# A decoder layer's attention: two heads' rotated scores side by side, and its rounds moved

## The reference

```
q = concatenate([q[..., :128], rope(q[..., 128:], positions)])
k = concatenate([k[..., :128], rope(k[..., 128:], positions)])
for j in range(4):                      # blocks of 128 queries, keys up to their end
    sc = einsum("bqhd,bkhd->bhqk", q[:, 128j:128j+128], k[:, :128j+128]) * 192 ** -0.5
    sc = where(k_chunk <= q_chunk, sc, -inf)          # chunks of 64
    out_j = softmax(sc) @ v[:, :128j+128]
```

## Time and profile before

| | us |
|---|---|
| median of three runs (2251.33 to 2252.22) | 2251.95 |
| the profiled execution, its own time | 2247.52 |
| its span, first to last instruction | 2245.6 |
| TensorE busy in the span | 2184.4 |
| attention rounds, 2093.3 to 2180.0: length, TensorE, VectorE, ScalarE | 86.7, 84.7, 66.4, 50.9 |
| output projection and store, 2180.0 to 2245.6: length, TensorE, VectorE | 65.6, 61.4, 31.2 |

### The profile page before, as it was taken

The page is one execution under the profiler, slowest core; times in us unless marked ns, Lnnn a source line. Parts: engine busy times, 40 slices in busy tenths (PEclk is TensorE's granted clock), DMA queues, the critical chain, the costliest instruction groups (busy, mean ns, idle before and its releaser), DMA issues. The chain is left out here.

```text
span 2245.6 us, 31402 instructions
## 1 busy us (share of the span) xinstructions
PE 2184.4 (97%) x11300; PEld 1575.4 (70%) x11300; DVE 1676.4 (75%) x2154; ACT 1392.2 (62%) x1805; POOL 341.0 (15%) x158
## 2 busy tenths in 40 slices
PE   8998989999999999999999999999999999999999
PEld 8987775556556555555556555677797787887777
DVE  6455658898898998898988998756655556885664
ACT  5344456777777777777777777754555455675553
POOL 3033130211220212220212200320000000320000
PEclk9999989999999999999999999999999999999999
DMA  6212349999999999999999999522221131131301
GB/s 183 78 58 94 110 171 343 371 383 384 375 378 375 373 382 384 373 381 376 374 383 387 367 382 373 206 81 89 80 71 57 57 136 37 51 134 38 113 1 38
DMA packets 179654, 506.85 MB, mean 226 GB/s; under 512 B 12541, under 2 KB 57373, under 8 KB 179565
## 3 DMA queue, kind: packets, MB, share of 16 engines
q1 hardware_dynamic: 174813, 494.92, 59.2%
q0 software_dynamic: 4752, 10.75, 2.2%
HBM read 492.99 MB, written 10.48 MB: 224 GB/s over the span
## 5 line engine op out<-in xcount | busy, mean ns | idle before, releaser
L2010 DVE TENSOR_TENSOR pieces_low<-pieces,pieces_high 128x2048 fp32r<-128x2048 f32 x383 | 873.3, 2289 | 110.5 <-ACT pieces_high L1958 105.7
L1958 ACT ACTIVATE pieces_high<-pieces 128x2048 fp32r<-128x2048 f32 x381 | 727.1, 1916 | 238.9 <-PE ps L1882 238.8
L1882 PE MATMUL ps<-pieces_high,ex_x 128*66 128x512 f32 x2080 | 575.9, 394 | 1.9 <-DVE ex_x L2044 1.5
L1882 PEld LDWEIGHTS ps<-pieces_high,ex_x 128*66 128x66 f32 x2080 | 279.9, 137 | 195.9 <-issue 6.9
L1882 PE MATMUL ps<-pieces_low,ex_x 128*66 128x512 f32 x1040 | 324.1, 393 | 0.0
L1882 PE MATMUL ps<-pieces_high,ex_h 128*66 128x512 f32 x992 | 277.4, 394 | 0.0
L483 DVE TENSOR_TENSOR in_w<-ring,in_w 128x256 fp32r<-128x256 f32 (+3 forms) x284 | 135.2, 483 | 161.6 <-ACT in_w L470 159.6
L2321 PE MATMUL ps<-hn_split,in_w 128*128 128x512 f32 (+1 forms) x888 | 227.3, 406 | 5.8 <-DVE hn_split L483 3.2
L1882 PEld LDWEIGHTS ps<-pieces_low,ex_x 128*66 128x66 f32 x1040 | 141.9, 136 | 97.7 <-issue 0.8
L470 ACT ACTIVATE in_w<-ring 128x256 fp32r<-128x256 f32 (+3 forms) x284 | 118.4, 419 | 131.9 <-PE ps L2321 58.6
L1882 PEld LDWEIGHTS ps<-pieces_high,ex_h 128*66 128x66 f32 x992 | 133.7, 136 | 90.7 <-DVE pieces_low L2010 3.2
(11 more groups left out here) (477 smaller groups left out, 2754.7 us busy)
## 6 DMA issues: line engine op xcount, KB each, us to landing
pieces<-in_w_gate SPq DMA_DIRECT2D x128, 1024.0 KB, 7.3
pieces<-in_w_up SPq DMA_DIRECT2D x128, 1024.0 KB, 7.5
pieces<-in_w_down SPq DMA_DIRECT2D x128, 1024.0 KB, 8.8
ring<-in_a_w_in SPq DMA_DIRECT2D x24, 1024.0 KB, 5.1
ring<-in_w_in SPq DMA_DIRECT2D x8, 1024.0 KB, 5.0
ring<-in_b_w_in SPq DMA_DIRECT2D x4, 2048.0 KB, 7.8
ring<-in_b_w_out SPq DMA_DIRECT2D x2, 3072.0 KB, 14.0
ring<-in_w_in SPq DMA_DIRECT2D x8, 512.0 KB, 3.5
```

Of the source, the lines that this page charges most:

```text
L1882: ins = pe.matmul(ps[0:CAP, banks + c, :], parts[a][:, k0 + k, :], w[b][:, k, c * 512:(c + 1) * 512], start=start and k == 0 and a == b == ...
L1958: nc.scalar.activation(m.high[:, n % NSPLIT, :], m.pieces[:, n % NPIECE, :], ACT.Copy).then_inc(high_done, 1)
L2010: nc.vector.tensor_tensor(m.low_part[:, n % NSPLIT, :], m.pieces[:, n % NPIECE, :], m.high[:, n % NSPLIT, :].bitcast(F32), ALU.subtract).t ...
```

## The change

- `qpt` has one tile per two heads, without zero rows; its clearing and the waits for that are gone, and `take_turned_pe` is one copy of 128 partitions.
- The causal units are ordered by two heads, then tile, then head of the two, so that units 2q and 2q+1 have the same tile of neighbouring heads. In an even round TensorE issues both plain scores, in the odd round after it both rotated scores, on 64 rows each, one on partitions 0 to 63 and one on 64 to 127; only these raise `scored`.
- There are four banks for scores (0, 1, 2, 7), and six buffers of weights. `turn` comes at u-4 instead of u-3, `values` at u-5 instead of u-4, `take` at u-6 instead of u-5, ScalarE's copy at u-4.
- The first three output splits are in rounds 33, 37 and 41 instead of 44, 46 and 48. Step 0 of the projection comes at the end of round 49, step 1 in round 50 before `values`, step 2 at the end of round 51, the rest last.

```diff
@@ -2144,16 +2144,16 @@
             final.g.pool_lows(pool)
 
 
-def attention_stage(m, name, units, at, y, x, out_slots, store):
+def attention_stage(m, name, units, at, st_at, y, x, out_slots, store):
 
 
 
     nc, ps = m.nc, m.ps
 
-    NB = 5
+    NB = 6
     probs = m.area(f"{name}_probs", [P, NB, 512], at)
     pt = m.area(f"{name}_pt", [P, 2, 512], at + 2048 * NB)
-    st = m.area(f"{name}_st", [P, NB, 4], at + 2048 * (NB + 2))
+    st = m.area(f"{name}_st", [P, NB, 4], st_at)
     scored = m.sem(f"{name}_scored")
     maxed = m.sem(f"{name}_maxed")
     exped = m.sem(f"{name}_exped")
@@ -2164,15 +2164,17 @@
     taken = m.sem(f"{name}_taken")
     nu = len(units)
 
-    whole = {k: [(taken, 16 + 4 * (k + 1))] for k in range(BH)}
-    bank_waits = {u % 3: [(exped, u + 1)] for u in range(nu - 3, nu)}
+    score_banks = (0, 1, 2, 7)
+    bank_of = lambda u: score_banks[u % 4]
+    whole = {k: [(taken, 16 + 8 * (k // 2 + 1))] for k in range(BH)}
+    bank_waits = {bank_of(u): [(exped, u + 1)] for u in range(nu - 4, nu)}
     bank_waits.update({i: [(pt_ready, nu)] for i in (3, 4)})
     bank_waits.update({i: [(taken, nu)] for i in (5, 6)})
     out = out_gemm(m, "out3", y, x, TILES2, out_slots, whole, banks=8,
-                   bank_order=[7] + [u % 3 for u in range(nu - 3, nu)] + [3, 4, 5, 6],
+                   bank_order=[bank_of(u) for u in range(nu - 4, nu)] + [3, 4, 5, 6],
                    bank_waits=bank_waits)
 
-    split_at = {nu - 4 + 2 * i: i for i in range(out.ns)}
+    split_at = {nu - 15 + 4 * i: i for i in range(out.ns)}
 
     with nc.Block() as block:
         @block.sync
@@ -2183,13 +2185,19 @@
         @block.tensor
         def _(pe):
             def scores(u):
-                if u >= 3:
-
-                    pe.wait_ge(exped, u - 2)
-                for i, (lhs, rhs) in enumerate(units[u]["scores"]):
-                    ins = pe.matmul(ps[:, u % 3, 0:units[u]["width"]], lhs, rhs,
-                                    start=(i == 0), stop=(i == len(units[u]["scores"]) - 1))
-                ins.then_inc(scored, 1)
+
+                if u >= 4:
+                    pe.wait_ge(exped, u - 3)
+                lhs, rhs = units[u]["scores"]
+                alone = "turned" not in units[u]
+                ins = pe.matmul(ps[:, bank_of(u), 0:units[u]["width"]], lhs, rhs, start=True, stop=alone)
+                if alone:
+                    ins.then_inc(scored, 1)
+
+            def turned_scores(u):
+
+                lhs, rhs = units[u]["turned"]
+                pe.matmul(ps[:, bank_of(u), 0:units[u]["width"]], lhs, rhs, start=False, stop=True).then_inc(scored, 1)
 
             def turn(u):
                 pe.wait_ge(ready, u + 1)
@@ -2210,16 +2218,26 @@
                                     start=(s == 0), stop=(s == len(vs) - 1))
                 ins.then_inc(summed, 1)
 
-            for u in range(nu + 4):
-                if u < nu:
+            for u in range(nu + 5):
+                if u < nu and "turned" not in units[u]:
                     scores(u)
-                if 3 <= u < nu + 3:
-                    turn(u - 3)
-                if u >= 4:
-                    values(u - 4)
-                if u == nu:
+                elif u < nu and u % 2 == 0:
+                    scores(u)
+                    scores(u + 1)
+                elif u < nu:
+                    turned_scores(u - 1)
+                    turned_scores(u)
+                if 4 <= u < nu + 4:
+                    turn(u - 4)
+                if u == nu + 2:
+                    out.products(pe, start=1, stop=2)
+                if u >= 5:
+                    values(u - 5)
+                if u == nu + 1:
                     out.products(pe, stop=1)
-            out.products(pe, start=1)
+                if u == nu + 3:
+                    out.products(pe, start=2, stop=3)
+            out.products(pe, start=3)
 
         @block.vector
         def _(dve):
@@ -2228,7 +2246,7 @@
             def head(u):
                 w = units[u]["width"]
                 dve.wait_ge(scored, u + 1)
-                s = ps[:, u % 3, 0:w]
+                s = ps[:, bank_of(u), 0:w]
                 if units[u]["mask"] is not None:
                     step(nc.vector.tensor_tensor(s[:, w - P:w], s[:, w - P:w], units[u]["mask"], ALU.add))
                 nc.vector.tensor_reduce(st[:, u % NB, 0:1], s, AX.X, ALU.max, negate=True).then_inc(maxed, 1)
@@ -2245,11 +2263,11 @@
                 y = units[u]["y"]
                 nc.vector.tensor_tensor(y, ps[:, 5 + u % 2, 0:P], y, ALU.mult).then_inc(taken, 1)
 
-            for u in range(nu + 5):
+            for u in range(nu + 6):
                 if u < nu:
                     head(u)
-                if u >= 5:
-                    take(u - 5)
+                if u >= 6:
+                    take(u - 6)
                 if 1 <= u <= nu:
                     norm(u - 1)
                 if u in split_at:
@@ -2258,10 +2276,10 @@
 
         @block.scalar
         def _(act):
-            for u in range(nu + 3):
-                if u >= 3:
-
-                    n = u - 3
+            for u in range(nu + 4):
+                if u >= 4:
+
+                    n = u - 4
                     w = units[n]["width"]
                     act.wait_ge(turned, n + 1)
                     if n >= 2:
@@ -2273,7 +2291,7 @@
                     act.wait_ge(maxed, u + 1)
                     if u >= NB:
                         act.wait_ge(turned, u - NB + 1)
-                    nc.scalar.activation(probs[:, u % NB, 0:w], ps[:, u % 3, 0:w], ACT.Exp,
+                    nc.scalar.activation(probs[:, u % NB, 0:w], ps[:, bank_of(u), 0:w], ACT.Exp,
                                          bias=st[:, u % NB, 0:1], accum_out=st[:, u % NB, 1:2]).then_inc(exped, 1)
                 if u in split_at:
                     out.highs(act, split_at[u])
...
@@ -3238,9 +3255,9 @@
                     nc.scalar.activation(qt[:, 2 * c + i, :], ps[:, 5 + i, :], ACT.Copy, scale=m.col("q_nope"))
 
             def take_turned_pe(c):
-                act.wait_ge(cleared, 1 if c == 0 else 2)
-                nc.scalar.activation(qpt[0:64, 2 * c, :], ps[0:64, 7, :], ACT.Copy)
-                nc.scalar.activation(qpt[64:128, 2 * c + 1, :], ps[64:128, 7, :], ACT.Copy).then_inc(q_taken, 1)
+                if c == 2:
+                    act.wait_ge(*used_after(QUP + NB - 1))
+                nc.scalar.activation(qpt[:, c, :], ps[:, 7, :], ACT.Copy).then_inc(q_taken, 1)
 
             def squares_mq():
                 act.wait_ge(*taken(MQ))
@@ -3446,8 +3463,6 @@
             def scale(x, r):
                 return tt(x, x, r.unsqueeze(3).to_broadcast(list(x.shape)), ALU.mult)
 
-            nc.gpsimd.memset(qpt[:, 0:2, :], 0.0).then_inc(cleared, 1)
-
             pool.wait_ge(r["spread_taken"], 1)
             pool.wait_ge(g.low, g.low_count(2 * KD))
             for k in range(KD):
@@ -3456,10 +3471,6 @@
                 pool.wait_ge(k_inverse, c + 1)
                 scale(kn[c % 2][:], ks[:, 2]).then_inc(k_scaled, 1)
             for c in range(NB):
-                if c == 2:
-
-                    pool.wait_ge(*used_after(QUP + NB - 1))
-                    nc.gpsimd.memset(qpt[:, 2:BH, :], 0.0).then_inc(cleared, 1)
                 pool.wait_ge(q_inverse, c + 1)
                 scale(q[c % 2][:, :, :, 0:NOPE], qss[:, 2]).then_inc(q_scaled, 1)
             pool.wait_ge(mq_inverse, 1)
@@ -3607,16 +3618,18 @@
         v = m.area("v3", [P, 4, BH, NOPE], 32768)
         y = m.area("y3", [P, 12, SEQ], 49152)
         kpt = m.area("kpt", [P, BH // 2, SEQ], 73728)
-        qpt = m.area("qpt", [P, BH, SEQ], 81920)
+        qpt = m.area("qpt", [P, BH // 2, SEQ], 81920)
         latent_stage(m, x, xt, kt, kpt, qt, qpt, v, y, mqt, m.gaps + [m.arena + 98304])
         m.close()
         units = memory_units(mqt, mk[1], mv[1], y)
-        for hd in range(BH):
+        for two in range(BH // 2):
             for t in range(4):
-                c, w = slice(t * P, (t + 1) * P), (t + 1) * P
-                units.append(dict(scores=[(qt[:, hd, c], kt[:, hd, 0:w]), (qpt[:, hd, c], kpt[:, hd // 2, 0:w])],
-                                  width=w, mask=m.chunk, values=[v[:, s, hd, :] for s in range(t + 1)],
-                                  y=y[:, hd, c]))
+                for i in range(2):
+                    hd, d = 2 * two + i, slice(64 * i, 64 * i + 64)
+                    c, w = slice(t * P, (t + 1) * P), (t + 1) * P
+                    units.append(dict(scores=(qt[:, hd, c], kt[:, hd, 0:w]), turned=(qpt[d, two, c], kpt[d, two, 0:w]),
+                                      width=w, mask=m.chunk, values=[v[:, s, hd, :] for s in range(t + 1)],
+                                      y=y[:, hd, c]))
         result_stored = m.sem("result_stored")
 
         def store_result(sp, g):
...
```

(5 more changed lines are left out.)

## The result

The changed kernel takes 2261.68 us (median of six runs, 2258.70 to 2263.09) against 2251.47 for the kernel before: 1.0048 times as long (1.0036 to 1.0059), 10.2 us slower. Run again beside the later experiments it was 1.0055 (1.0041 to 1.0068). The profiled execution took 2262.86, its span is 2261.0. TensorE's busy time is hardly changed, yet the span is 15.4 us longer.

What follows compares the result with a forecast made beforehand. TensorE was taken to bound the kernel, so its stream and waits count in full. The terms for scores, waits, tail, start and stage before sum to +13.4 us on 2252.0, giving 2265.4; range 2257 to 2271.

Steps and rivals of the forecast that it cites:

- Scores, -2.4: Rotated scores, two heads at once on 64 rows: 8.7 us saved, less 16 visits at 0.39 (6.3), leaves -2.4.
- Odd rounds, +15.6: Causal attention: TensorE stands before values until VectorE has done mask, maximum and take; 3.82 us a cycle, 15.6 in all.
- the forecast's rule: Odd-round wait: 1.43 to 1.03 us by the new pair's blocks, less transposes of the pair two before (0.11 to 0.44).
- Even rounds behind four blocks, +1.2: Where four blocks are followed by one, values(2q-3) waits for take(2q-5) behind head(2q+1): 0.4 us, three times.
- The tail, +3.0: End of attention: projection step 3 waits 1.9 us for splits behind the last take; with values(43) and values(44), 3.0.
- The waits of before, -2.6: Four TensorE waits around the output splits go: 1.6 us idle plus 0.25 at each place, 2.6 saved.
- Start, +0.4: Filling the pipe: first copy of turned weights stands behind one more exponential, values start 0.85 later, 0.4 us lost.
- The stage before, -1.8: Stage ahead of attention: one ScalarE copy of 128 partitions replaces two of 64, three times 0.59 us, 1.8 less.
- the takes are in time: Rival: take done before values need it, so no wait appears; -4.3 us, 2247.7, faster; 8%.
- only ScalarE is late: Rival: only the copy for values(2q-3), behind exp(2q) in ScalarE's queue, comes late; 1.4 us a cycle, 2253; 6%.
- No running side by side: Rival: the two heads' rotated records don't run side by side, so the 8.7 us are not saved; 2274; 3%.
- The clock falls: Rival: TensorE's stands of about a microsecond per pair make its clock fall once per cycle, 7.6 us; 2273; 7%.

Runs made afterwards that it cites:

- both heads on the same rows: Changed kernel with both heads of a pair reading rotated parts from partitions 0 to 63, so nothing runs side by side; ratio 1.0038 to the kernel before.
- Take first: Changed kernel with take(u-6) before head(u) instead of behind it in each VectorE round; 2252.20 us, ratio 1.0009 to the kernel before.
- take before the maximum: Changed kernel with take(u-6) between the mask and the maximum of head(u); ratio 1.0035 to the kernel before.
- the balanced order: Changed kernel with key sizes ordered 1, 2, 4, 3 blocks instead of 1, 2, 3, 4; ratio 1.0042 to the kernel before.
- The splits placed earlier: Changed kernel with take ahead of head, ScalarE's copies before the exponential, and splits of steps 3 and 4 in rounds nu+2 and nu+3; ratio 1.0001.
- 64 rows one at a time: Kernel before, its rounds kept, with packed qpt and each unit's rotated score alone on 64 rows behind its plain score; 2256.69 us, ratio 1.0027.

## Why the prediction was right

The mechanism and the sign held; the median lies 3.7 below the 2265.4 forecast. By its steps, all of them in the attention stage except the last:

- *Scores, -2.4.* Measured -3.1: a visit costs 0.345 (0.20 in, 0.15 out) and not 0.39, 5.5 for sixteen. The step left out what the run with both heads on the same rows showed of it: the 8.7 saved aren't worth anything while TensorE stands behind the pair.
- *Odd rounds, +15.6.* Measured 16.6: 4.4 in the first cycle and 4.06 in each of the others, every stand 0.05 to 0.07 longer than worked out (0.76, 0.79, 1.24, 1.27 for 0.70, 0.72, 1.19, 1.21); for the two beside memory units the forecast had 0.3 more, and they are 0.11 and 0.21 longer than the others of their kind. Take first removes all but one, take before the maximum shortens them by most of a maximum, and the balanced order changes each as the forecast's rule says.
- *Even rounds behind four blocks, +1.2.* Measured 3 x 0.44 = 1.3.
- *The tail, +3.0.* values(43) stands 0.89, step 3 of the projection 1.87, values(44) 0.16 at most: 2.8 to 2.9. The splits placed earlier take the 1.87 away.
- *The waits of before, -2.6.* By the same count the trace of before has stands of 0.42, 0.64, 1.26 and 0.29 (at 2117.50, 2167.62, 2172.49 and 2177.64), 2.6 in all, and none of them is in the changed kernel. What the other measured terms leave of +15.2 is -2.7. No experiment takes them away by themselves.
- *Start, +0.4.* Measured 1.45 us of stands against 1.10 before: +0.35.
- *The stage before, -1.8.* -2.0 (from the first transposes of kn, 1949.96 before and 1950.40 after, to those of the weights, 145.8 and 143.8). The third place that I had named, the splits at 2025.6, didn't gain at all; one further stand of 0.7 went away instead.

Added up for the attention stage the forecast is +15.2, and the two traces show +15.2 and +15.4. What came out too high is the sum for the median: with the 2.0 of the stage before the sum is 13.2 to 13.4, and the timed ratios say 10.8 (8.1 to 13.3) and 12.4 (9.2 to 15.3). A part of the gap is shown below: the packed `qpt` is worth 3.4 us and not 2.0 in eight of the eleven traces that have it, since a clock fall goes with it. What then stays, about one us, is within the intervals, and I leave it open. So it was luck that the profiled execution, one of the three with the fall, gave -2.0 for the -1.8 forecast; most give -3.4.

The rivals: *the takes are in time* (2247.7) and *only ScalarE is late* (2253) are out by the releasers in the trace and by the experiment with take first. That experiment comes near to making the second rival true: 2252.2, where it had said 2253. In part this is luck, since the rival had four places of 1.4 and nothing for the split of round 37. *No running side by side* is out: the four records of 512 columns take 1.13 us, not 1.98. *The clock falls* is out: of the two traces of the changed kernel one has a fall among the attention rounds and the projection, in the tail, for 1.7 us, and not one in each cycle.

## What to carry to other kernels

When work for two units is merged so that both finish together, look for each engine's queue at what it does between the first unit's results and the things the producer needs back: here one take behind a mask and a maximum cost 16 us of stands, and changing the order of two lines gave 10.7 us of the stage back and about 9 by the timed ratios. When results come a round later, what the producer needs back must be queued ahead of the work on them; to make the values a round later still, or to give them a third bank, is the other way, and wasn't tried here. A saving upstream of a stand is worth nothing until the stand is gone (8.7 us of stream were added, and the time stayed the same), and side work such as the splits belongs beside small units: moving them, those of the tail among them, gave 3.8 us of the stage.

## What the runs showed of the hardware

**A visit to 64 rows** costs TensorE 0.20 us going in and 0.15 coming out, the same for 128 to 512 columns (64 rows one at a time), and the same with two heads side by side (the changed kernel).

**The clock.** The same kernel, with the same stands to 0.01 us, had its granted clock fall in one execution and not in the other. First the changed kernel, then the same again, over the same stretch of the tail (the third number from the end is the granted clock):

```profile
2183.00:2186.00 3.00, 3.00 (x15) 2.90 (x16) 1.46 (x6) 1.19 (x4) 0.00 (x0) 0.51 0.03 5
```

```profile
2183.00:2186.00 3.00, 3.00 (x16) 2.46 (x15) 0.00 (x0) 0.60 (x1) 0.00 (x0) 1.00 0.00 0
```

0.51 is the lower of the two levels, 1.2 of 2.4 GHz, nearly throughout. Up to TensorE's last matmul, the attention stage had such a fall in 4 of the 14 profiled executions, each time within a few us of a stand of 0.9 to 1.9 us, and it cost 1.5 to 1.7 us. Sixteen stands of about one us brought at most one.

In the stage before, behind a stand of 2.3 us, it came in all three executions of kernels with full-row qpt (once 40 us earlier, behind a stand of 2.0), and in three of eleven with the packed one, though the stand of 2.3 is there in all of them. The changed kernel, and the same again:

```profile
2032.00:2036.00 4.00, 3.47 (x9) 2.75 (x10) 3.01 (x5) 0.00 (x0) 0.00 (x0) 0.61 0.00 0
```

```profile
2031.00:2035.00 4.00, 3.50 (x15) 2.93 (x16) 2.97 (x5) 0.45 (x1) 0.00 (x0) 1.00 0.00 0
```

The stage takes 145.8 to 146.0 us with full rows, 143.8 to 143.9 packed with the fall, 142.3 to 142.5 packed without. Whether shorter stands at the transposes of q (1.33 and 0.82 in the changed kernel instead of 1.97 and 1.42) are what keeps the clock up wasn't tried, and the packed traces speak against it: the three with the fall have the shortest first stand of the eleven (1.33 to 1.34), the eight without it 1.37 to 1.60.
